# High parts of the products first, a quarter of the weights ahead of the second tile's turn, other order of the first loads

## The reference

```python
# first block
h = rmsnorm(x, norm1_w)
rq, rk, rv, rg, mq, mk, mv, ga, gb = split(h @ w_in)
a = (silu(rg) * retention(rotary(rq), rotary(rk) * 128**-0.5, rv)) @ w_ret_out
b = moba_attention(rmsnorm(mq), rmsnorm(mk), mv) @ w_moba_out
x = x + (sigmoid(ga) * a + sigmoid(gb) * b) @ w_o
h2 = rmsnorm(x, norm2_w)
x = x + (silu(h2 @ w_ffn_gate) * (h2 @ w_ffn_up)) @ w_ffn_down
# second block, layers i = 0, 1
if i == 1: k_nope, k_rope, v = shared_kv(x)       # x @ w_down, rms_norm, rope, c_kv @ w_up
x = layer_norm(alpha * x + 0.5 * swiglu(x))       # every swiglu is 2816 wide
x = layer_norm(alpha * x + (fox_mixer(x) if i == 0 else mla_mixer(x)))
x = layer_norm(alpha * x + 0.5 * swiglu(x))
x = layer_norm(alpha * x + sigmoid(x @ w_gate + b_gate) * (p[i] @ w_proj))
```

## Time and profile before

| what | us |
|---|---|
| median of three runs | 1600.09 (1599.52 to 1602.39) |
| profiled execution | 1599.46 |
| its span, first to last instruction | 1597.4 |
| TensorE busy in it | 1522.3 (95%) |
| VectorE, ScalarE, GpSimd busy | 945.2, 784.9, 184.7 |
| mean granted clock of TensorE | 0.985 of full speed |

### The profile page before, as it was taken

One profiled execution on the slowest core, in us unless ns is written; L12 is line 12 of the kernel. 1 busy time (PEld: TensorE's weight loads), 2 busy tenths in 40 slices (PEclk: granted clock), 3 DMA queues, 4 the chain that ended last, 5 costly groups with the idle time before them and its releaser, 6 DMA issues.

```text
span 1597.4 us, 22028 instructions
## 1 busy us (share of the span) xinstructions
PE 1522.3 (95%) x8440; PEld 1323.6 (83%) x8440; DVE 945.2 (59%) x1213; ACT 784.9 (49%) x935; POOL 184.7 (12%) x52
## 2 busy tenths in 40 slices
PE   6999999999999999899899999799998899999997
PEld 5887888888888887798788888788888788888885
DVE  4566365666556666414566667766566454666667
ACT  4436545444444445555454445554445463544445
POOL 2014211000010001350100001100004332100001
PEclk9999999999999999899999999899999999999999
DMA  7545445665555554533455555565554233565552
GB/s 278 187 131 174 140 158 185 211 193 190 190 182 195 195 185 142 162 120 99 139 197 196 186 184 187 166 210 187 196 188 143 82 128 135 162 222 195 184 197 79
DMA packets 187003, 274.87 MB, mean 172 GB/s; under 512 B 9968, under 2 KB 137072, under 8 KB 186864
## 3 DMA queue, kind: packets, MB, share of 16 engines
q1 hardware_dynamic: 182848, 261.72, 49.5%
q10 hardware_dynamic: 4096, 12.32, 2.5%
HBM read 272.96 MB, written 1.05 MB: 172 GB/s over the span
## 4 chain that ended last, share of the span: by engine, by line
PE 83%; DVE 10%; ACT 4%; issue 1%; POOL 1%; DMA 1%; ACTq 0%; SPq 0%; DVEq 0%
PE bank L592 22%; PE bank L594 11%; PE bank L502 9%; PE bank L504 9%; PE bank L503 9%; PE acc L502 6%; PE acc L503 6%; PE acc L504 6%; DVE w_lo L1462 2%; ACT w_hi L1035 2%; PE acc L709 2%; PE acc L498 2%; DVE x L1513 1%; DVE x L1564 1%; POOL w_lo L459 1%
## 5 line engine op out<-in xcount | busy, mean ns | idle before, releaser
L1462 DVE TENSOR_TENSOR w_lo<-w_raw,w_hi 128x2048 fp32r<-128x2048 f32 (+2 forms) x209 | 477.5, 2285 | 217.7 <-ACT w_hi L1111 121.5
L592 PE MATMUL bank<-xT,w_hi 128*128 128x512 f32 x1520 | 379.9, 392 | 0.0
L459 POOL TENSOR_TENSOR w_lo<-w_raw,w_hi 128x2048 fp32r<-128x2048 f32 (+2 forms) x43 | 180.6, 4202 | 1379.4 <-ACT w_hi L1035 1379.4
L592 PEld LDWEIGHTS bank<-xT,w_hi 128*128 128x128 f32 x1520 | 276.1, 189 | 51.4
L1111 ACT ACTIVATE w_hi<-w_raw 128x2048 fp32r<-128x2048 f32 x145 | 276.4, 1906 | 0.0
L502 PE MATMUL bank<-w_hi,xT 128*128 128x512 f32 (+1 forms) x624 | 232.9, 373 | 19.3 <-DVE xT L1503 12.5
L1035 ACT ACTIVATE w_hi<-w_raw 128x2048 fp32r<-128x2048 f32 (+4 forms) x107 | 194.2, 1817 | 97.9 <-PE bank L504 76.7
L504 PE MATMUL bank<-w_hi,xT 128*128 128x512 f32 (+1 forms) x624 | 228.2, 366 | 0.0
L503 PE MATMUL bank<-w_lo,xT 128*128 128x512 f32 (+1 forms) x624 | 228.0, 365 | 0.0
L594 PEld LDWEIGHTS bank<-xT,w_lo 128*128 128x128 f32 x1520 | 207.4, 190 | 14.8
L594 PE MATMUL bank<-xT,w_lo 128*128 128x256 f32 x1520 | 211.9, 282 | 0.0
(11 more groups left out here) (192 smaller groups left out, 1870.7 us busy)
## 6 DMA issues: line engine op xcount, KB each, us to landing
w_raw<-in_ffn_w_in SPq DMA_DIRECT2D x176, 512.0 KB, 4.4
w_raw<-in_ffn_w_out SPq DMA_DIRECT2D x88, 512.0 KB, 4.1
w_raw<-in_w_in SPq DMA_DIRECT2D x52, 512.0 KB, 4.8
w_raw<-in_fox_w_in SPq DMA_DIRECT2D x24, 512.0 KB, 4.6
w_raw<-in_w_ffn_gate SPq DMA_DIRECT2D x22, 512.0 KB, 4.5
w_raw<-in_w_ffn_up SPq DMA_DIRECT2D x22, 512.0 KB, 4.5
w_raw<-in_w_ffn_down SPq DMA_DIRECT2D x22, 512.0 KB, 4.1
w_raw<-in_ple_w_gate SPq DMA_DIRECT2D x16, 512.0 KB, 4.1
```

The source lines that it names most:

```text
L459: pool.tensor_tensor(w_lo[slot][:, 0:cols], w_raw[slot][:, 0:cols], w_hi[slot][:, 0:cols].bitcast(F32), ALU.subtract).then_inc(w_lo_done[s ...
L592: pe.matmul(out, wh[:, k, m], both, start=k == 0, stop=False)
L1462: nc.vector.tensor_tensor(w_lo[slot][:, 0:cols], w_raw[slot][:, 0:cols], w_hi[slot][:, 0:cols].bitcast(F32), ALU.subtract)\
```

## The change

It does five things.

1. `Chunk.run` (where the chunk belongs to a turn) and `first` of the feed-forward part no longer call `mm3` slice by slice. For a unit and a tile they issue all high by high matmuls, waiting only for "xTh" and `w_hi`; then, in a first unit, the high by low ones (after a wait for `w_lo`) and the low by high ones (after "xT"); in a second unit those two in the other order. The number of matmuls stays.
2. The first half (by slices) of the second unit for tile 0 moves from behind tile 1's transposes to ahead of them, at the sites 0, 2, 4, 5, 8 (`early` in `tile_steps`) and in four of the five starts of a feed-forward part (`start`); the start without a turn gets the same order.
3. Site 6: PE runs `kv(0)` ahead of the turn of tile 0 and `kv(1)` between the two turns. ACT runs `keep_kv(0)` ahead of the copies of tile 0's turn (`filler`) and `keep_kv(1)` ahead of those of tile 1. DVE makes `w_lo` of dq0's first unit within the second tile's finish.
4. Start: SP issues x tile 0, unit 0, x tile 1, unit 1, unit 2, then the constants. Unit 1's `w_lo` moves from POOL to DVE, after the scaling of tile 1 and ahead of its `xTl`.
5. The first norm's gains come as one row of 4 KB; PE spreads them into two banks by two fp32 matmuls with a row of ones, and DVE reads them there.

```diff
-    pool_units |= {unit_at[stage][i] for stage, i in (("rq0", 1), ("rg0", 1), ("moba_out1", 0), ("fox_v4", 1),
+    pool_units |= {unit_at[stage][i] for stage, i in (("rg0", 1), ("moba_out1", 0), ("fox_v4", 1),
...
             for t in range(T):
                 sp.dma_start(x[:, t], dram["x"][t * P:(t + 1) * P, :]).then_inc(x_loaded[t], 16)
-            u = 0
+                load(t)
+            u = 2
...
-                if u == 2:
+                if u == 3:
                     for name, dst in CONSTS:
...
+                                stop = w == last and js[-1] == kt - 1
+                                pe.wait_ge(w_hi_done, u + 1)
+                                for j in js:
+                                    need("pe", "xTh", self.ready, t, (k0 + j) // 4)
+                                    pe.matmul(out, self.ah[:, self.slot0 + k0 + j, tok], wh[:, j, cols],
+                                              start=w == 0 and j == 0, stop=False)
+
+                                def rest_of_weights(stop):
+                                    pe.wait_ge(w_lo_done[u % RING], u // RING + 1)
...
+                                def rest_of_x(stop):
+                                    for j in js:
+                                        need("pe", "xT", self.ready, t, (k0 + j) // 4)
...
+                                if w:
+                                    rest_of_x(False)
+                                    mm = rest_of_weights(stop)
+                                else:
+                                    rest_of_weights(False)
+                                    mm = rest_of_x(stop)
...
-                return [lambda: c.run(0, tiles=(0,)), lambda: c.run(1, tiles=(0,)), lambda: c.run(0, 1, tiles=(1,))]
+                def early():
+                    c.run(0, tiles=(0,))
+                    c.run(1, tiles=(0,), part=0)
+
+                return [early, lambda: c.run(1, tiles=(0,), part=1), lambda: c.run(0, 1, tiles=(1,))]
...
                     first(0, 0)
+                    first(1, 0, range(KD // 2))
...
-                for b, t in ((1, 0), (0, 1), (1, 1)):
-                    first(b, t)
+                first(1, 0, range(KD // 2, KD))
+                for b in range(2):
+                    first(b, 1)
...
+            pe.wait_ge(ones_set, 1)
+            pe.wait_ge(gb_loaded, gb_count(0))
+            for q in range(2):
+                take(2 + q, ("norm", 0, 1, 1))
+                mm = pe.matmul(bank[2 + q], ones, gain_row[:, q * CH:(q + 1) * CH], start=True, stop=True)
...
-                    to_xT(6, x, b0=4, between=lambda: kv(0))
+                    kv(0)
+                    to_xT(6, x, b0=4, between=lambda: kv(1))
...
-                    kv(1)
                     chunk("dq0", (4, 5), ready=6)
...
-            load_norm(0)
+            act.dma_start(gain_row, dram["norm1_w"].rearrange("(a n) -> a n", a=1)).then_inc(gb_loaded, 16)
...
-                    norm_and_turn(6, early=split[0] + 1, between=lambda: keep_kv(0), b0=4)
+                    norm_and_turn(6, early=split[0] + 1, filler=lambda: keep_kv(0), between=lambda: keep_kv(1), b0=4)
...
                 if t:
                     split_to(1)
-
-            norm_and_turn(0, x_tile, rms=True, b0=4)
+                dve.wait_ge(x_loaded[t], 16)
+
+            norm_and_turn(0, x_tile, rms=True, b0=4, late=lambda: split_to(2))
...
+                def finish_half(t):
+                    add_half(t)
+                    if l and t:
+                        split_to(unit_at["dq0"][0] + 1)
```

More of the change, by code:

```diff
@@ L516, in __init__, with run @@
                     self.kts = [units[u][1] for u in self.us]
-                def run(self, *which, tiles=range(T)):
+                def run(self, *which, tiles=range(T), part=None):
                     last = len(self.us) - 1
                     for t in tiles:
-                        if which[0] == 0:
+                        if which[0] == 0 and part != 1:
                             take(self.banks[t], ("ev", *self.name, t))
@@ L532, in run @@
                             cols = slice(c0, c0 + min(n, CH))
[L533 to L540, removed]
+                            out = bank[self.banks[t]][:, 0:cols.stop - cols.start]
@@ L541, in run @@
+                            if part == 0:
+                                continue
                             if t == 0 and w == last:
@@ L605, in last_up, with first, rest_of_weights, rest_of_x @@
                     mm.then_inc(w_used, 1)
-                def first(b, t):
+                def first(b, t, ks=range(KD)):
                     u = u0 + b
-                    if t == 0:
-                        pe.wait_ge(w_lo_done[u % RING], u // RING + 1)
[L613 to L618, removed]
+                    wh, wl = (w[u % RING][:, :].rearrange("p (k n) -> p k n", k=KD) for w in (w_hi, w_lo))
+                    tok, out = slice(t * P, (t + 1) * P), bank[2 * b][:, t * HB:(t + 1) * HB]
+                    pe.wait_ge(w_hi_done, u + 1)
+                    for k in ks:
+                        need("pe", "xTh", site, t, k // 4)
+                        pe.matmul(out, xTh[:, k, tok], wh[:, k], start=k == 0, stop=False)
+                    def rest_of_weights(stop):
+                        pe.wait_ge(w_lo_done[u % RING], u // RING + 1)
+                        for k in ks:
+                            mm = pe.matmul(out, xTh[:, k, tok], wl[:, k], start=False, stop=stop and k == KD - 1)
+                        return mm
+                    def rest_of_x(stop):
+                        for k in ks:
+                            need("pe", "xT", site, t, k // 4)
+                            mm = pe.matmul(out, xTl[:, k, tok], wh[:, k], start=False, stop=stop and k == KD - 1)
+                        return mm
+                    if b:
+                        rest_of_x(False)
+                        mm = rest_of_weights(True)
+                    else:
+                        rest_of_weights(False)
+                        mm = rest_of_x(True)
                     if t == 1:
@@ L1081, in root, with norm_and_turn @@
                 go(("std", site, t), std[:, t:t + 1], sq_sum[:, t:t + 1], ACT.Sqrt, bias=eps[:, e:e + 1], scale=1.0 / D)
-            def norm_and_turn(site, rms=False, first=None, early=None, between=None, b0=0):
+            def norm_and_turn(site, rms=False, first=None, early=None, filler=None, between=None, b0=0):
                 squares_sum(site, 0, rms)
@@ L1091, in norm_and_turn @@
                     split_to(early)
+                if filler is not None:
+                    filler()
                 if site < 9:
@@ L1552, in inverse @@
                     did(nc.vector.reciprocal(rstd[:, t:t + 1], std[:, t:t + 1]))
-                    if rms and t == 0:
+                    if site == 0:
+                        need("dve", "gain0")
+                    elif rms and t == 0:
                         dve.wait_ge(gb_loaded, gb_count(site))
@@ L1583, in norm_and_turn @@
                 apply(1, 1)
+                if late is not None:
+                    late()
                 rest(1, 0)
```

34 lines of the change are left out of this document (27 added, 7 removed).

## The result

| | before | after |
|---|---|---|
| median, us | 1599.84 (1599.52 to 1602.39, 4 runs) | 1578.03 (1577.2 to 1579.92, 4 runs) |
| ratio, with its 95% interval | | 0.9861 (0.9849 to 0.9874) |
| span of the profiled execution | 1597.4 | 1575.1 |
| mean granted clock | 0.985 | 0.990 |

21.8 us less, where 14.55 were forecast and the range ended at 1581.5. The direction was right, the size was not.

The account below looks back on a forecast made before the run. The prediction took TensorE as the bound (83% of the chain of waits). Its terms, 4.7 + 2.95 + 1.4 + 0.9 + 4.6 = 14.55 us, gave 1585.5 us; the range over its rivals was 1581.5 to 1591.8.

Parts of the forecast that it names:

- Start, 4.7: First product rq0: earlier landing of unit 0, DVE in POOL's place and the half unit ahead end it 4.7 us earlier.
- the landing's 2.7 us: At the start: unit 0 lands at 8.3 instead of 11.02 with fewer bytes ahead, 2.7 us of the gain.
- The lower end, 7.0 for the landing: Earliest landing of unit 0 considered, 7.0 us, without the 0.49 MB of later loads moving beside it; start gain then 6.0.
- Four feed-forward starts, 2.95: Sites 1, 3, 7 and "raw": high part first lets PE start on ACT's copy before DVE's low part; 2.95 us less.
- Site 2, 1.4: Ahead of tile 1's turn, held by DVE: PE does 6 matmuls there that are gone behind it; 1.4 us less.
- Site 5, 0.9: kv_down and ffn3's first units: high part and half unit go ahead of late low parts; 0.9 us less.
- Site 6, 4.6: kv(0) fills the 4.69 us wait, dq0 ends 5.2 earlier, and cq comes at 1238.0; 4.6 us less.
- cq's wait: Sign for the new profile: PE's wait for the normed cq, 3.56 us before, still near 4 us.
- A: Rival at the start: unit 0's landing does not move, 2.7 us less gain, 1588.2 us; chance 0.12.
- B: Rival at site 6: POOL goes first, delaying DVE's second dq0 low part; cq 1.3 later, 1591.4 us; chance 0.09.
- C: Rival on PE's clock: new gaps bring half-clock drops costing 1.7 us each, 1589 to 1590.6, or 1582.3; chance 0.10.
- D: Rival in the reordered matmuls: sweeps cost more than slices; 18 ns more each cancels the gain, 29 ns gives 1609; chance 0.03.

Follow-up runs that it names:

- dq0 alone: High part first in dq0 only, on the kernel before with part 3: 1590.38 us; dq0 back to slices, on the changed kernel: 1585.02 us.
- POOL waiting: POOL subtracts kv_up's unit 3 only after DVE has normed cq, on the kernel before: 1594.66 us; the same with part 3: 1588.97 us.
- POOL's work doubled: POOL's subtraction of uq's unit 0 done twice, on the changed kernel: 1585.83 us.

## Why the prediction was wrong

- **Start, 4.7, measured 6.1: right mechanism, one size off.** Of the landing's 2.7 us the x tile's part was about right (1.33 measured). The gains were priced by their bytes at the common rate, 1.35 us, and took 2.40. The lower end, 7.0 for the landing, was nearly met. A slip of 0.14 is in the sum itself: the first of the 36 matmuls takes 0.34 us, so that rq0 ended at 30.83 before, not 30.69. 2.3 of the 6.1 are DVE in POOL's place and the high part first; the half unit, which the forecast counted in here, gave nothing measurable. The matmuls of ones took 3.74 us, more than the 3 allowed for, and ended at about 6.1, just ahead of DVE's need: hidden, as forecast.
- **Four feed-forward starts, 2.95: right at three.** Each wait of 1.07 to 1.14 is 0.34, 0.73 less where 0.74 was forecast, but two of the three keep it by the half unit alone, which the forecast priced at nothing there. Site 3 was sized from a wait at half clock (0.72) and is worth 1.4 to 1.5 at either pattern of the clock.
- **Site 2, 1.4: right** (1.3), and the part has a second use there: without it the gap is long enough for the clock to fall behind it.
- **Site 5, 0.9: about right** (0.8 at the product's start, 0.6 once ffn3 goes on; the order of its first units gives nothing more).
- **mla_ob0: overlooked.** `tile_steps` is used there without a turn of x. The half unit delays the last turn of the attention by 1.9 us and the wait of 1.41 behind it stays: 0.56 lost.
- **Site 6, 4.6, measured 10.7: the step that failed** is "POOL's three units follow ACT and one another: ... kv_up 3 to 1235.5; DVE then needs its last 2.5: cq at 1238.0, 4.6 less". dq0's end was sized right (5.2 forecast, 5.8 measured). But kv_up's unit 3 does not follow uq's: its load is released by dq0's second low part and takes 8 us, so its subtraction begins 2.95 us after uq's ends, and the root fits in between. cq's wait did not stay near 4 us, it vanished: 3.56 us, and 1.3 more, most of it from the half clock that had followed it. My own list of queues did not hold SP's load, though the low part whose lateness I had noted is what releases it. The runs with dq0 alone (5.4 and 7.0 us), with POOL waiting (5.3 and 6.8) and with POOL's work doubled (7.8) show the step three ways. That the change fell on the good side was luck: no part of it was aimed at the root, and the margin is 0.8 us.
- **The rivals.** A did not come (the landing moved by 3.8 us). B did not come, but its mechanism decides the result with the other sign. The rule of the Trainium skill that was weighed ("SBUF — State Buffer", Who interferes with whom) says that a DVE instruction with two SBUF inputs and a GpSimd one exclude each other; by that rule the rows agree at 1233.03, 1222.69 and 652.26. The same section counts a tensor_scalar in a 2-port mode among the instructions that can contend, and two steps of the root with a single source agree: the one of 2.54 us in the run with POOL's work doubled, and the root's first, which takes 1.24 us at 1234.15 above and ends within 0.03 us of POOL's subtraction. C's half-clock stretches came and went (118 and 756 new; 630, 780, 1210 and 1241 gone), on the whole for the better. D did not come: four matmuls of a sweep take 0.91 us at full clock (19.26 to 20.17 in the first product), 0.227 each, as the slices do.

The sum of what was measured: 6.1 + 2.3 (sites 1, raw, 7) + 1.5 (site 3) + 1.3 + 0.6 + 10.7 - 0.56 + 0.3 (clock at 118 and 654) = 22.2 of 22.3.

## What to carry to other kernels

When two engines exclude each other, what counts is in which order they arrive; write down for both what releases them (the load behind the slot as well), and see how far they are apart. A short chain whose margin is 0.1 us before or under 1 us after should be made safe by an order, even by a wait on the engine that has time. And a part that pays 4 us alone can pay 12 or 13 beside another: undo each part from both ends before crediting it.

## What the runs showed of the hardware

- A POOL subtraction stretches DVE operations of 128x2 and 16x256 numbers to 4.5 and 4.7 us, not only large ones; those with two sources in SBUF, and the root's TENSOR_SCALARs of 128x2 with one, pay to POOL's end when they arrive while POOL runs. Beside POOL a sum of x with a PSUM bank (128x512) keeps its 0.69 us and a TENSOR_SCALAR of 128x1 its 0.21 (1200.15 and 1200.88 in the kernel before).
- 0.52 MB spread from one row of 4 KB to 128 partitions delayed the next load by 2.40 us, 0.52 MB of x by 1.33, one profile each, with a landing that varies by up to 0.75 us.
- The place of a half-clock stretch can differ between two executions of one program (the changed kernel: one at 118 us and none at site 6, or the other way round), and between kernels with the same instructions so far (766 or 780 us, three profiles each, with the same time from there to 974 within 0.3 us), although two profiles of the kernel before agree in all of them to the microsecond.
